# A first stage in which two projection chunks are multiplied quarter by quarter between the modulation pieces

## The reference, cut to what matters

```
mod_x = silu(c) @ w_ada + b_ada          # shift, scale, gate: 6 parts of 2048
mod_c = silu(c_ctx) @ w_ada + b_ada
h  = rmsnorm(x,   norm1_w) * (1 + s1)  + sh1      # 256 tokens
hc = rmsnorm(ctx, norm1_w) * (1 + s1c) + sh1c     # 256 context rows
p  = h @ w_in ; pc = hc @ w_in           # 3776 columns: q, k, v, c_q, c_kv, k_rope
```

## Time and profile before

| | us |
|---|---|
| median of 3 runs | 2905.84 |
| lowest, highest | 2901.80, 2914.29 |
| span of the profiled execution, first to last instruction | 2899.2 |
| busy PE, DVE, ACT, POOL in it | 2796.0, 1763.7, 1232.5, 167.1 |
| mean granted TensorE clock | 0.992 of full |

### The profile page before, as it was taken

One profiled execution on the slowest core, in us unless ns is written; L12 is line 12 of the kernel. 1 busy time (PEld: TensorE's weight loads), 2 busy tenths in 40 slices (PEclk: granted clock), 3 DMA queues, 4 the chain that ended last, 5 costly groups with the idle time before them and its releaser, 6 DMA issues.

```text
span 2899.2 us, 34323 instructions
## 1 busy us (share of the span) xinstructions
PE 2796.0 (96%) x13474; PEld 2286.3 (79%) x13474; DVE 1763.7 (61%) x1959; ACT 1232.5 (43%) x1345; POOL 167.1 (6%) x340
## 2 busy tenths in 40 slices
PE   6899998999999999999999999999999999999998
PEld 3587865677888888888888888888788888888877
DVE  2586777875655555555765567985755455545554
ACT  4232216643544434435465443434644444434333
POOL 0000215100000000000000000016300000000000
PEclk9999999999999999999999999999999999999999
DMA  9798975774545565546757776667266555556554
GB/s 395 285 331 284 313 264 192 269 290 146 195 163 182 203 216 189 171 163 211 226 192 252 244 225 220 224 193 207 87 197 210 189 194 189 178 192 203 166 175 152
DMA packets 348574, 621.44 MB, mean 214 GB/s; under 512 B 49792, under 2 KB 102672, under 8 KB 340896
## 3 DMA queue, kind: packets, MB, share of 16 engines
q1 hardware_dynamic: 311568, 586.76, 60.1%
q10 hardware_dynamic: 36880, 32.94, 3.4%
HBM read 590.64 MB, written 29.00 MB: 214 GB/s over the span
## 4 chain that ended last, share of the span: by engine, by line
PE 87%; DVE 4%; DMA 3%; ACT 2%; issue 1%; SPq 1%; POOL 1%; ACTq 0%; DVEq 0%; POOLq 0%
PE ps L309 23%; PE ps L311 23%; PE ps L310 23%; PE ps L1187 3%; PE ps L1188 3%; PE ps L1189 3%; DMA raw<-in_pack_ada 1%; DVE w_lo L271 1%; PE ps L414 1%; PE ps L1864 1%; DMA ctx_in<-in_ctx 1%; DMA k_in<-proj 1%; DVE w_lo L958 1%; PE ps L1473 0%; PE ps L326 0%
## 5 line engine op out<-in xcount | busy, mean ns | idle before, releaser
L271 DVE TENSOR_TENSOR w_lo<-raw,w_hi 128x2048 fp32r<-128x2048 f32 (+3 forms) x428 | 896.1, 2102 | 671.9 <-ACT w_hi L264 670.4
L264 ACT ACTIVATE w_hi<-raw 128x2048 fp32r<-128x2048 f32 (+3 forms) x428 | 747.4, 1757 | 733.9 <-PE ps L311 685.2
L309 PE MATMUL ps<-w_hi,a_hi 128*128 128x512 f32 x2240 | 877.1, 392 | 2.8 <-DVE a_lo L795 2.2
L311 PE MATMUL ps<-w_hi,a_lo 128*128 128x512 f32 x2240 | 872.4, 389 | 0.0
L310 PE MATMUL ps<-w_lo,a_hi 128*128 128x512 f32 x2240 | 871.9, 389 | 0.0
L309 PEld LDWEIGHTS ps<-w_hi,a_hi 128*128 128x128 f32 x2240 | 420.6, 188 | 89.5 <-DVE a_lo L795 2.7
L311 PEld LDWEIGHTS ps<-w_hi,a_lo 128*128 128x128 f32 x2240 | 420.4, 188 | 87.8
L310 PEld LDWEIGHTS ps<-w_lo,a_hi 128*128 128x128 f32 x2240 | 420.7, 188 | 85.7
L309 PE MATMUL ps<-w_hi,b_hi 128*128 128x512 f32 x796 | 312.4, 392 | 3.6 <-DVE b_lo L834 3.6
L311 PE MATMUL ps<-w_hi,b_lo 128*128 128x512 f32 x796 | 310.5, 390 | 0.0
L310 PE MATMUL ps<-w_lo,b_hi 128*128 128x512 f32 x796 | 310.4, 390 | 0.0
(11 more groups left out here) (373 smaller groups left out, 2758.1 us busy)
## 6 DMA issues: line engine op xcount, KB each, us to landing
raw<-in_hyb_w_in SPq DMA_DIRECT2D x96, 1024.0 KB, 5.7
raw<-in_sc_w_in SPq DMA_DIRECT2D x96, 1024.0 KB, 5.1
raw<-in_w_up SPq DMA_DIRECT2D x88, 1024.0 KB, 5.0
raw<-in_pack_ada SPq DMA_DIRECT2D x96, 512.0 KB, 6.1
raw<-in_w_down SPq DMA_DIRECT2D x48, 768.0 KB, 4.3
raw<-in_w_in SPq DMA_DIRECT2D x24, 1024.0 KB, 7.5
raw<-in_hyb_w_out SPq DMA_DIRECT2D x32, 768.0 KB, 4.5
raw<-in_sc_w_out SPq DMA_DIRECT2D x32, 768.0 KB, 4.4
```

Source lines behind the costliest of these rows:

```text
L264: nc.scalar.activation(w_hi[s][:, 0:n_k, 0:ncols], raw[s][:, 0:n_k, 0:ncols], ACT.Copy).then_inc(sem("hi_done"), 1)
L271: nc.vector.tensor_tensor(w_lo[s][:, 0:n_k, 0:ncols], raw[s][:, 0:n_k, 0:ncols], w_hi[s][:, 0:n_k, 0:ncols].bitcast(F32), ALU.subtract).th ...
L309: nc.tensor.matmul(o, h, w_hi[s][:, k, 0:ncols], start=kt == 0, stop=False)
L311: last = nc.tensor.matmul(o, l, w_hi[s][:, k, 0:ncols], start=False, stop=kt == L.groups[-1][0] + L.groups[-1][1] - 1)
```

## The change

Only the first stage and the order of the first eight dense pieces are touched.

- Flips: all eight token flips stand behind modulation piece 2 on PE, all eight context flips behind piece 5, over six PSUM banks (0 to 5). ACT copies the eight token flips before it squares the context. The forms alternate token, context, token, context.
- Sums: banks 6 and 7 in turn; a total is written into the bank of its sum.
- Dense: K0 and QL are multiplied together, quarter by quarter. In each quarter eight K steps (four of K0, four of QL, in turn) stand behind modulation pieces 10 to 17, 19 to 26 and 27 onwards; the fourth quarter is whole pieces 6 and 7. A piece waits for half of its quarter's forms at its first K tile and for the other half at its third.
- Ring: from piece 10 on, two of the five modulation buffers are those of the tokens `X` (reloaded later, in attention, as before).
- Late units: none behind pieces 4 to 6, seven behind piece 7, three behind 8, 9 and 10; the same from piece 11 on.

```diff
-        LATE_AFTER = [0] * 4 + [2, 3, 3, 2, 2, 2, 2, 3, 3, 3, 4, ...
+        LATE_AFTER = [0] * 7 + [7, 3, 3, 3, 3, 3, 3, 4, ...
+        ADA_IN_X = 10
+        ada_in_x = [place(f"ada_x{t}", [P, GROUP, CHUNK], at=X0 + t * PIECE_BYTES) for t in range(TILES)]
+        def ada_home(n):
+            r = n % ADA_RING
+            return ada_in_x[r - 2] if n >= ADA_IN_X and 2 <= r < 2 + TILES else ada_ring[r]
...
+            if n == ADA_IN_X + 2:
+                sp.wait_ge(sem("flip_t"), KT // 2)
...
-            dense_after = {7: 0, 13: 1, 20: 2, 26: 3}
+            dense_after = {5: 0, 8: 1, 13: 2, 16: 3, 21: 4, 24: 5, 29: 6}
...
+        def ada_bank(M):
+            return 6 + M % 2
...
             if g == 0 and M >= 2:
-                pe.wait_ge(sem("mrow"), M - 1)
+                pe.wait_ge(sem("cols_out"), M - 1)
...
-            if j:
-                pe.wait_ge(sem("z_done"), j)
+            if f >= Z_BANKS:
+                pe.wait_ge(sem("z_done"), f - Z_BANKS + 1)
...
-            dve.wait_ge(sem("z_done"), j + 1)
+            dve.wait_ge(sem("z_done"), KT)
...
         def ada_pe(pe):
+            def dense(q, i):
+                proj_piece(pe, 2 * q + i % 2, (i // 2,))
+            for n in range(8):
                 ada_first(pe, n)
+                if n == 2:
+                    for f in range(KT // 2):
+                        z_flip(pe, f)
+                if n == 4:
+                    ada_total(pe, 0)
+                if n == 5:
+                    for f in range(KT // 2, KT):
+                        z_flip(pe, f)
+            ada_total(pe, 1)
+            steps = {n: (q, n - first) for q, first in enumerate((10, 19, 27)) for n in range(first, first + 8)}
+            for n in range(8, N_FIRST):
+                ada_first(pe, n)
+                if n in steps:
+                    dense(*steps[n])
+                if n % RING == 0 and n > 8:
                     ada_total(pe, n // RING - 1)
+            dense(2, 5)
             ada_total(pe, N_ADA - 1)
+            for i in (6, 7):
+                dense(2, i)
+            for p in (6, 7):
+                proj_piece(pe, p)
...
             norm_stats_act(act, "n1", [X[:, t, :] for t in range(TILES)], D, 0)
+            for f in range(KT // 2):
+                z_copy(act, f)
             act.wait_ge(sem("ctx_in"), 32)
             norm_stats_act(act, "n1c", [ctx_in[t][:] for t in range(TILES)], D, 2)
...
+            for f in range(KT // 2, KT):
+                z_copy(act, f)
+            for quarter in range(4):
+                proj_hi(act, 2 * quarter)
                 for j in range(4 * quarter, 4 * quarter + 4):
                     h_high(act, j)
+                proj_hi(act, 2 * quarter + 1)
...
+            for quarter in range(4):
+                if quarter:
+                    ada_copy(dve, 2 * quarter)
+                    ada_out(dve, chain, 2 * quarter)
+                proj_lo(dve, 2 * quarter)
+                ada_copy(dve, 2 * quarter + 1)
+                ada_out(dve, chain, 2 * quarter + 1)
+                forms(4 * quarter, 4 * quarter + 4)
+                proj_lo(dve, 2 * quarter + 1)
+            dve.wait_ge(sem("flip_lo"), KT)
+            for p in range(FIRST_PIECES):
+                for n in units_after(p):
+                    late_unit(dve, chain, n)
...
-        PIECES = [(K0, 0), (K0, 1), (K0, 2), (QL, 0), (QL, 1), (K0, 3), (QL, 2), (QL, 3)] + [
+        FIRST_PIECES = 8
+        PIECES = [(j, g) for g in range(4) for j in (K0, QL)] + [
...
-                    pe.wait_ge(sem("flip_lo"), 4 * (g + 1))
+                    pe.wait_ge(sem("flip_lo"), 4 * g + 2)
...
+                if j in (K0, QL) and k == 2:
+                    pe.wait_ge(sem("flip_lo"), 4 * g + 4)
```

More of the change, by code:

```diff
@@ L422, in ada_total @@
                 pe.wait_ge(sem("cols_in"), 16 * 4)
-            else:
-                pe.wait_ge(sem("cols_out"), M)
             for b in range(CT):
-                last = nc.tensor.matmul(ps[:, 6, 2 * b:2 * b + 2], mrow[M % 2][:, b * P:(b + 1) * P], sel2[:], start=True, stop=True)
+                last = nc.tensor.matmul(ps[:, ada_bank(M), 2 * b:2 * b + 2], mrow[M % 2][:, b * P:(b + 1) * P], sel2[:], start=True, stop=True)
             last.then_inc(sem("msum"), 1)
@@ L474, in z_flip, with z_copy @@
                     src = ctx_in[t][:, c] if of_ctx else X[:, t, c]
-                    last = nc.tensor.transpose(ps[:, 7, (k * TILES + t) * P:(k * TILES + t + 1) * P], src, ident[:])
+                    last = nc.tensor.transpose(ps[:, f % Z_BANKS, (k * TILES + t) * P:(k * TILES + t + 1) * P], src, ident[:])
             last.then_inc(sem("flip_t"), 1)
-        def z_copy(act, j):
-            act.wait_ge(sem("flip_t"), j + 1)
-            nc.scalar.activation(z_tile(j).rearrange("p k s -> p (k s)"), ps[:, 7, :], ACT.Copy).then_inc(sem("z_done"), 1)
+        def z_copy(act, f):
+            kt = 2 * f % KT
+            z = (z_c if f >= KT // 2 else z_x)[:, kt:kt + 2, :]
+            act.wait_ge(sem("flip_t"), f + 1)
+            nc.scalar.activation(z.rearrange("p k s -> p (k s)"), ps[:, f % Z_BANKS, :], ACT.Copy).then_inc(sem("z_done"), 1)
         def h_split(j):
@@ L564, in ada_dve @@
         def ada_dve(dve, chain):
-            for b in (4, 5):
-                nc.vector.memset(ps[:, b, :], 0.0)
+            for M in range(2):
+                nc.vector.memset(ps[:, ada_bank(M), :], 0.0)
             nc.vector.memset(C["eps"], EPS)
@@ L917, in proj_sp @@
         def proj_sp(sp):
-            proj_load(sp, 4)
             for n in range(LATE_SLOTS):
                 late_load(sp, n)
-            for p in range(3, N_PROJ):
+            for p in range(FIRST_PIECES - RAW_PROJ - 1, N_PROJ):
                 if p + RAW_PROJ < N_PROJ:
@@ L1064, in proj_act @@
         def proj_act(act):
-            for p in range(4, N_PROJ + 4):
+            for p in range(FIRST_PIECES, N_PROJ + 4):
                 if p == N_PROJ:
@@ L1193, in proj_pe @@
         def proj_pe(pe):
-            for p in range(3, N_PROJ):
+            for p in range(FIRST_PIECES, N_PROJ):
                 proj_piece(pe, p)
```

74 lines of the change are left out of this document (14 added, 60 removed).

## The result

The kernel after takes 2907.59 us (median of 20 runs, 2901.71 to 2912.65), the kernel before on the same chip 2902.56 (20 runs, 2898.25 to 2914.29). The ratio is 1.0016, with a 95% interval of 1.001 to 1.0023: slower by 0.16%, 5.0 us in the medians. That is less than the half per cent that the forecast took for no change, but these 20 runs tell it from none. The profiled span went from 2899.2 to 2902.8 us.

What follows compares the result with a forecast made beforehand. PE and DVE both full before V0, whose start hangs on DVE; PE leads afterwards. V: +6.2 (F), -5.3 (low halves), +1.5 (total), -1.0 (load wait) = +1.4, taken as +1: span 2900.2, plus 6.6, hence 2907 us; range 2895 to 2915.

Steps and rivals of the forecast that it cites:

- likeliest case: The time range held likeliest by itself, 2902 to 2911 us; the forecast, V between -3 and +5, had chance 0.62.
- F: End of the last forms on DVE, 131.2 us before; forecast at 137.4, 6.2 us later.
- V0: The value chunk on PE; its start, V, was 193.1 us before and forecast about 1 us later, near 194.
- T: End of the context flips on PE; forecast at 47 us (45.1 to 48.0), with the context ready at 39.8.
- So KL can start on PE only at F + 14.6 = 152.0: KL's start behind DVE's 2.4 us for `w_lo(7)`, 10.7 for seven units and 1.45 for `w_lo(8)`.
- the wait for the first late total: DVE's unit 16 reuses that total's row: wanted at 173.9, total out at 175.4; new wait 1.5 us (0 to 1.9).
- rival C: DMA starves the seven late units behind F, costing from nothing to 3 us; B with C had chance 0.25.
- The wait of 6 us ahead of the latent flip: At KL's third piece, PE arrives at 166.4 and idles 6 us until DVE has scaled the latents at 172.4.
- A shift of V0 is kept to the end: From V0 on PE leads again, DVE idling 8.97 us ahead of 229.48, so V0's shift reaches the end.
- signs of being wrong: V0 before 188, DVE pausing over 3 us between F and V, or the time changing behind V0.
- A: PE decides and its saved work is kept: KL at 150.8, V 10 us earlier, 2896 us; chance 0.13.
- B: Bunched PE waits bring the low clock: F 5 to 6 us later, V about +6.5, 2912 us; with C 0.25.

## Why the prediction came out as it did

The forecast (2907.0 us, slower by about 1) and the time (2907.59) lie within a microsecond, and the time is inside the likeliest case's range. Most of that is luck, twice over. The forecast stood on a median of three runs of before, 2905.84, and twenty runs give 2902.56: the kernel was slower by 5.0 us, not by 1. And in the working two errors of opposite sign, -3.8 us at F and +8.3 us from F to V0, cancel in part.

F moves by itself from execution to execution. To take that out, the table counts from F (read as the start of the first low half behind the last forms, less the idle time before it; one execution each, us):

| | F | KL less F | V0 less F |
|---|---|---|---|
| forecast | 137.4 | 14.6 | 56.7 |
| before | 131.17 | 29.81 | 61.95 |
| before, K0 copied at piece 10 | 133.77 | 33.83 | 65.02 |
| after | 133.64 | 28.94 | 65.00 |
| K0 copied at piece 8 | 134.71 | 20.61 | 58.99 |
| the same, units 4, 4, 4, 4 | 134.40 | 14.15 | 57.86 |

**T and F: mechanism right, a size off.** The waits were forecast at 5.3 and 3.4 us and came as 5.53 and 3.70. The eight token flips were costed at about 8 us, "mostly low", from a price of 1.03 us for a single flip, and took 5.40: they started at the low pace as forecast, but in a row a low flip takes 0.86 us (ACT's copies of them start at 23.90, 24.76 and 25.61), and from 26.2 us on the pace was nearly twice as high (last section). So the context was ready at 37.4 and not 39.8, T was 43.95 and not 47, and F came at 133.6 (134.64 less 1.00), where 137.4 was forecast and before had 131.2. From T to F the working gave 90.4 us and the trace 89.7; 3.1 of the 3.8 us are in T. Even the 2.5 us between before and after at F are not sure: the kernels whose first stage is that of before have 130.75, 131.17 and 133.77.

**"So KL can start on PE only at F + 14.6 = 152.0": the step that failed.** It counted the low halves and the seven units and left out the copy of K0, which frees KL's accumulators. KL started at 162.58, F + 28.9. The row at 159.02 in the earlier trace rows was read as a length, 1.22 us, and not as something that the matmul 0.74 us behind its end needs. In before the copy came just in time, and there was no wait to point at it. The working even had the copy at 162.5, 10 us behind its own start of KL, and did not ask who waits. The change did not make the copy late: it starts 27.6 us behind F, in before 27.9. It took work of PE's away from ahead of KL, left the copy where it was, and put the late total, which stood ahead of KL, behind two of its pieces. The Trainium skill, "PSUM — Partial Sum Buffer", section "Summary: rules for kernel authors", says to evacuate promptly because the memory is tight; here the price of not doing so is what moving the copy gives back, 4.9 us at V0.

**F to V.** Forecast 56.7 us, measured 65.0 (133.64 to 198.64). Two terms make 7.9 of the 8.3 us: the wait for the first late total, forecast 1.5 and measured 7.10, since KL, and with it the total in its queue, was late; and DVE's waits for unit loads, 1.31 + 0.39 + 0.59 = 2.3, where the sum had nothing (rival C gave 0 to 3). The wait of 6 us ahead of the latent flip did not come in after, because PE arrived late itself. With the copy moved and the units spread it came, 7.30 us, and there the rest of the working comes out too: KL at F + 14.15 for 14.6, V0 at F + 57.86 for 56.7. The sum for DVE was right but for the step above.

**V0.** Forecast +1.0, measured +5.5: less 3.8 for F, plus 8.3 from F on. Counted from F, V0 was to come 5 us sooner than in before and came 3 us later. "A shift of V0 is kept to the end" held to 316 us and then only in part: at 387 a shorter wait took 3 us back. Two of the prediction's own signs of being wrong came true: DVE paused for 7.10 us between F and V, and the time changed behind V0.

**Rivals.** A (PE's saved work is kept, V0 10 us earlier) is refuted: with KL 12 us earlier than in before, V0 moved by 0.9, or by 4.1 counted from F, less even than the 5.3 that the working took off DVE's queue. B (the clock) named the right condition, waits ahead of flips and total 1 beyond 3 us, but F was 3.8 earlier than forecast and not 5 to 6 later. C was right in kind and size.

**Open.** Where the last 1.8 us between 387 us and the end stem from, and why the write out of `stg` took 7.75 us instead of 5.49.

## What to carry to other kernels

Before moving work ahead, list for each accumulator who frees it and in whose queue the freeing instruction stands; a copy that came just in time before shows no wait, and becomes the bound as soon as PE arrives earlier. Move the copy with the matmuls. Where a wait of PE's has no named releaser, look for a copy out of PSUM that ends about 0.1 us ahead of it. And work that is moved in a table takes with it everything keyed to the same index (here totals and column outputs): a shift that is right for the next 60 us can make PE and DVE wait for each other in turn behind them.

## What the hardware showed that was not expected

The length of a group of matmuls is a mean, and it can hide a change of clock inside the group; the column of the granted clock did not show it here. In after the 32 transposes of the token flips took 5.40 us, 0.67 for four, which is what a single flip took at the high clock in before. A modulation piece ahead of them ran at the low length, 1.88 us against the 1.04 of the piece behind them:

```profile
17.29 1.88 PE L426 MATMUL ps<-ada_h,condf 128*2 128x512 f32 x8 [3.55 <-DMA ada_h<-in_pack_ada]
...
28.08 1.04 PE L426 MATMUL ps<-ada_l,condf 128*2 128x512 f32 x8
```

Read as a mean, this looks as if the flips, after an idle time of 3.58 us, had been fast from the start. Two windows inside them show otherwise (stretch, its length, busy time and number of instructions of PE, PEld, DVE, ACT and POOL, then granted clock, DMA share, GB/s):

```profile
25.00:26.20 1.20, 1.20 (x7) 1.20 (x6) 0.00 (x0) 0.94 (x2) 0.00 (x0) 1.00 1.02 423
26.20:27.40 1.20, 1.20 (x13) 1.20 (x12) 0.00 (x0) 0.97 (x3) 0.00 (x0) 1.00 1.05 437
```

Up to 26.2 us PE got through 7 transposes in 1.2 us, from there on through 13. The context flips, at a granted clock of 0.50, also made 7 in 1.2 us (38.00 to 39.20), so the token flips began at the low clock, 1.2 GHz, and changed to the high one, 2.4 GHz, after PE had worked without a pause since 22.75. Yet the granted clock reads 1.00 in both windows, and 1.00 too at the piece at 17.29 with its low length. In this first part of the trace the lengths tell the clock and the column does not; later it does, with 0.50 at the context flips up to 43.0 us. Why it differs is not shown.
